# One change of three parts in a decoder step on one core: the projection's sample tile and taps, the order of the prompt attention, and the padded rows of the experts

## Time and profile before

| what | us |
|---|---|
| median of 3 runs (lowest, highest) | 1763.69 (1761.9, 1769.64) |
| the profiled execution: its own time | 1765.26 |
| the profiled execution: its span | 1763.6 |
| TensorE busy in the span | 1430.2 (81%) |
| VectorE busy | 664.6 (38%) |
| ScalarE busy | 372.2 (21%) |
| GpSimd busy | 194.4 (11%) |

### The profile page before, as it was taken

One profiled execution on the slowest core, in us unless ns is written; L12 is line 12 of the kernel. 1 busy time (PEld: TensorE's weight loads), 2 busy tenths in 40 slices (PEclk: granted clock), 3 DMA queues, 4 the chain that ended last, 5 costly groups with the idle time before them and its releaser, 6 DMA issues. The chain is left out here.

```text
span 1763.6 us, 22716 instructions
## 1 busy us (share of the span) xinstructions
PE 1430.2 (81%) x7464; PEld 835.2 (47%) x7464; DVE 664.6 (38%) x1309; ACT 372.2 (21%) x795; POOL 194.4 (11%) x348
## 2 busy tenths in 40 slices
PE   5999989558899788824499942999999999999960
PEld 4665544257755555612355521445444544454430
DVE  3597676611378566635122255000110010010007
ACT  4000111212255555520111110111111111111113
POOL 0000011253100000013000000011111111111111
PEclk9999999778679999966699975899999999999985
DMA  7500000365330000045411103999999999999927
GB/s 261 226 1 6 12 15 21 104 224 175 96 97 25 1 1 1 1 125 144 159 48 72 39 17 132 379 411 394 408 408 406 400 412 411 406 394 408 406 104 291
DMA packets 83021, 336.99 MB, mean 191 GB/s; under 512 B 9834, under 2 KB 45803, under 8 KB 64834
## 3 DMA queue, kind: packets, MB, share of 16 engines
q1 hardware_dynamic: 65130, 287.76, 42.1%
q0 software_dynamic: 15440, 47.30, 7.8%
q10 hardware_dynamic: 2384, 1.06, 0.2%
HBM read 311.20 MB, written 29.45 MB: 193 GB/s over the span
## 5 line engine op out<-in xcount | busy, mean ns | idle before, releaser
L1752 PE MATMUL ps<-arena 128*128 128x512 f32 x544 | 239.8, 597 | 0.0
L1752 PEld LDWEIGHTS ps<-arena 128*128 128x128 f32 x544 | 102.0, 190 | 136.9 <-issue 136.8
L351 PE MATMUL ps<-arena 128*128 128x512 f32 (+3 forms) x432 | 158.9, 527 | 0.0
L504 DVE SCALAR_TENSOR_TENSOR arena<-arena 128x1024 f32<-128x1024 f32 x120 | 147.7, 1283 | 1.3
L1453 PE MATMUL ps<-arena 128*128 128x512 f32 (+1 forms) x288 | 129.4, 603 | 15.8 <-DVE arena L1548 15.8
L1806 PE MATMUL ps<-arena 128*128 128x512 f32 x272 | 120.1, 593 | 7.5 <-DMA arena<-scratch_h,ints 7.5
L1760 PE MATMUL ps<-arena 128*64 128x256 f32 x1088 | 121.2, 380 | 0.0
L306 PE MATMUL ps<-arena 128*128 128x352 f32 x384 | 116.5, 464 | 4.3 <-issue 3.8
L1053 ACT ACTIVATE arena<-ps,arena 128x640 f32<-128x640 f32 (+7 forms) x128 | 90.0, 703 | 119.8 <-DVE arena L1132 103.3
L351 PEld LDWEIGHTS ps<-arena 128*128 128x128 f32 (+1 forms) x432 | 77.2, 180 | 79.4 <-issue 72.0
L964 PE MATMUL ps<-arena 128*128 128x128 f32 x528 | 82.8, 287 | 35.7 <-ACT arena L1063 32.1
(11 more groups left out here) (357 smaller groups left out, 1543.7 us busy)
## 6 DMA issues: line engine op xcount, KB each, us to landing
arena<-in_w_gate SPq DMA_DIRECT2D x34, 2048.0 KB, 11.6
arena<-in_w_up SPq DMA_DIRECT2D x34, 2048.0 KB, 16.4
arena<-in_w_down SPq DMA_DIRECT2D x34, 2048.0 KB, 16.6
arena<-in_x_prompt SPq DMA_DIRECT2D x16, 512.0 KB, 6.5
arena<-in_cache_cmp SPq DMA_DIRECT2D x64, 128.0 KB, 2.7
arena<-in_cache_cmp POOLq DMA_DIRECT2D x64, 128.0 KB, 3.2
arena<-in_cache_sel SPq DMA_DIRECT2D x64, 128.0 KB, 2.1
arena<-scratch_y SPq DMA_DIRECT2D x16, 512.0 KB, 5.5
```

What stands on the lines that cost most here:

```text
L351: mm = pe.matmul(ps[:n, b + o // 512, 0:w], xT[:, k, t * P:t * P + n], w_tm[:, k, o:o + w], start=(k == 0), stop=(k == KT_ - 1))
L504: ins = dve.scalar_tensor_tensor(o, i, dw[:, c, j:j + 1], o, ALU.mult, ALU.add)
L1752: mm = pe.matmul(ps[:, bank, :], xgT_l[:, k, :], w[LARGE][:, k, :], start=(k == 0), stop=(k == KT_ - 1))
```

## The change

Projection: the sample tile's columns are cut into four quarters of 326, each made in its own 32-column tile of TensorE, all in one bank; ScalarE copies four pieces. The 62 late taps go behind seven tiles, nine each. The state rows are copied to a place of their own after all taps, and GpSimd stores them in the compression block between its page loads of quarter 1 and the additions. Attention: chunks and the transposes back share banks 4, 5 and 7 in turn, sums use bank 6 alone; the copier of a chunk is chosen so that each half has one large copy on one engine; ScalarE does both exps before `take(2p+1)`; VectorE masks and reduces one half, then the other. Experts: empty slots get an index past the bounds (8 x 1056), and the indirect DMAs leave such rows out; the token rows' places are set to zero once; TensorE raises the first semaphores at the start of the block.

```diff
+        QTR = COLS_TM // 4
...
+                    else:
                         for k in range(KT_):
-                            mm = pe.matmul(ps[:n, b + o // 512, 0:w], xT[:, k, t * P:t * P + n],
-                                           w_tm[:, k, o:o + w], start=(k == 0), stop=(k == KT_ - 1))
+                            for q in range(4):
+                                mm = pe.matmul(ps[n * q:n * q + n, b, 0:QTR], xT[:, k, t * P:t * P + n],
+                                               w_tm[:, k, QTR * q:QTR * q + QTR], start=(k == 0),
+                                               stop=(k == KT_ - 1), tile_position=(0, n * q))
...
+                        for q in range(4):
+                            m = min(QTR, 1280 - QTR * q)
+                            act.activation(p_sb[:n, t % 2, QTR * q:QTR * q + m], ps[n * q:n * q + n, b, 0:m], ACT.Copy)
+                        logit = ps[3 * n:4 * n, b, QTR - 24:QTR]
+                    act.activation(gates[:n, t, :], logit, ACT.Sigmoid).then_inc(sem("tm_copied"), 1)
...
-                act.wait_ge(sem("qk_turned"), TILES)
-                act.activation(xin[:TAPS - 1, 0, 0:512], ps[:TAPS - 1, 0, :], ACT.Copy)
-                act.activation(xin[:NB * NS, 1, 0:512], ps[:NB * NS, 1, :], ACT.Copy)\
+                act.wait_ge(sem("tapped"), 4 * TAPS)
+                act.wait_ge(sem("sample_tapped"), 4)
+                act.activation(state_p[:TAPS - 1], ps[:TAPS - 1, 0, :], ACT.Copy)
+                act.activation(state_s[:NB * NS], ps[:NB * NS, 1, :], ACT.Copy)\
                    .then_inc(sem("state_ready"), 1)
+                act.wait_ge(sem("state_ready"), 1)
...
-                share = -(-len(late_taps) // TILES)
+                share = -(-len(late_taps) // (NQ - 1))
...
                 cmp_pages(pool, 1, 1)
+                pool.dma_start(out["out8"], state_p[:TAPS - 1]).then_inc(sem("conv_out"), 16)
+                for s in range(NS):
+                    pool.dma_start(out["out9"][:, TAPS - 1 - NS + s, :], state_s[NB * s:NB * (s + 1)])\
+                        .then_inc(sem("conv_out"), 16)
                 pool.wait_ge(sem("conv_gain_in"), 48)
...
+        def turn_bank(kind, n):
+
+            return (4, 5, 7)[turn_place[kind, n] % 3]
...
-            if keys(h // 2) > 4:
-                return "dve" if o else "act"
-            return "act" if h % 2 else "dve"
+            return "dve" if (h % 2 == 0) == (o > 0) else "act"
...
-                        if c >= 2:
-                            pe.wait_ge(sem(f"pT_{copier(c - 2)}"), copied_by(copier(c - 2), c - 2))
+                        bank_free("chunk", c)
...
-                    if r == 0 and i > 0:
-                        pe.wait_ge(sem("combined"), 2 * (i - 1) + w + 1)
+                    if r == 0 and p > 0:
+                        pe.wait_ge(sem("out_copied"), p // R)
...
                     for q in scored_at(p):
                         exp(2 * q)
+                        exp(2 * q + 1)
                     take(2 * p + 1)
-                    for q in scored_at(p):
-                        exp(2 * q + 1)
...
                     for g in range(KV):
+                        h = 2 * p + g
...
-                        ins = dve.tensor_tensor(s[:, (m - 1) * P:m * P], s[:, (m - 1) * P:m * P], con("causal"), ALU.add)
-                    chain(ins)
-                    for g in range(KV):
-                        h = 2 * p + g
-                        dve.tensor_reduce(neg_max[:, h % 4:h % 4 + 1], scores(p, g), AX.X, ALU.max, negate=True)\
+                        chain(dve.tensor_tensor(s[:, (m - 1) * P:m * P], s[:, (m - 1) * P:m * P], con("causal"),
+                                                ALU.add))
+                        dve.tensor_reduce(neg_max[:, h % 4:h % 4 + 1], s, AX.X, ALU.max, negate=True)\
                            .then_inc(sem("max_ready"), 1)
...
                 pool.indirect_dma_start(into, None, scratch_h,
-                                        bass.IndirectOffsetOnAxis(ap=ids.bitcast(U32), axis=0))\
+                                        bass.IndirectOffsetOnAxis(ap=ids.bitcast(U32), axis=0),
+                                        bounds_check=TOKENS - 1, oob_is_err=False)\
...
-            for name in ("upped0", "upped1", "downed0", "downed1", "xg_turned0", "xg_turned1"):
-                pe.sem_inc(sem(name), 1)
...
             @block.tensor
             def _(pe):
+                for name in ("upped0", "upped1", "downed0", "downed1", "xg_turned0", "xg_turned1"):
+                    pe.sem_inc(sem(name), 1)
                 pe.wait_ge(sem("counted"), 1)
...
+                dve.memset(xg_l, 0.0)
+                chain(dve.memset(xg_s, 0.0))
                 dve.wait_ge(sem("table_made"), 1)
...
+                chain(dve.tensor_scalar(empty, ps[:, 2, COLS:2 * COLS], 0.0, 8.0 * TOKENS, ALU.is_equal, ALU.mult))
+                chain(dve.memset(empty[0:1, :], 0.0))
+                dve.tensor_tensor(ints[:, 0:2 * ROUNDS], empty, ps[:, 2, 0:COLS], ALU.add).then_inc(sem("table_ready"), 1)
```

More of the change, by code:

```diff
@@ L954, in score, with bank_free @@
                     mm.then_inc(sem("scored"), 1)
+                def bank_free(kind, n):
+                    place = turn_place[kind, n]
+                    if place >= 3:
+                        before, c = turn_order[place - 3]
+                        if before == "back":
+                            pe.wait_ge(sem("combined"), c + 1)
+                        else:
+                            pe.wait_ge(sem(f"pT_{copier(c)}"), copied_by(copier(c), c))
                 def turn(h):
```

69 lines of the change are left out of this document (43 added, 26 removed).

## The result

The changed kernel takes 1723.37 us (median of 4 runs, 1722.36 to 1727.85) against 1762.80 us (4 runs on the same chip, 1756.57 to 1769.64): a ratio of 0.9772, with a 95% interval of 0.9752 to 0.9791. Its profiled execution took 1724.38 us by its own time, with a span of 1722.5 (before: 1765.26 and 1763.6). The forecast was 1723 in a range of 1706 to 1744; the time fits, but in each of its three parts a step behind the number was wrong, in the attention most of all.

What follows compares the result with a forecast made beforehand. No single bound: TensorE in projection and experts, page loads in compression, a three-engine chain in wide attention. Gains 16.2 + 10.5 + 14.5 = 41.2 off 1765.3 give 1724.1; the runs' median stands 1.6 lower: 1723, range 1706 to 1744.

Steps and rivals of the forecast that it cites:

- Sample tile: Projection's end: four column tiles run side by side, products 4.6 us instead of 17.69, bounds 4.4 and 8.1; gain 13.1.
- Stores moved: Compression block: stores in GpSimd's queue delay later page loads and TensorE's waiting product; cost 2.9 us, bounds 0 and 3.5.
- net 16.2: Projection and what follows: next block 19.1 us earlier, less 2.9 for the moved stores.
- Attention: Whole attention block: 10.5 us gained, 8.5 in the wide and 2 in the narrow part.
- Wide attention: 32 wide pairs: shorter chain gains 10.9 us, VectorE late behind copies and combines takes 2.4 back; net 8.5.
- Narrow attention: Narrow pairs: a third bank takes only the few waits for a copy; gain 2 us, bounds -2 and 5.
- Experts, start: Start of experts: weights asked for near 1066, gathers landed near 1100; products 8 us sooner, bounds 3 and 12.
- Experts, padding: Expert rounds: a third fewer rows shorten transfers some 3 us; 6.5 of 7.5 us of waits go, bounds 0 and 7.5.
- Attention nothing: Rival, attention: VectorE's extra copy and the combine eat the 0.34 us per pair; 1733 us, chance 0.13.
- Experts keep their waits: Rival, expert rounds: fixed transfer time keeps the 6.5 us of waits, 8 gained instead of 14.5; 1730 us, chance 0.11.
- no side by side: Rival, sample tile: quarters run in turn and the tile stays at 17.7 us; 1736 us, chance 0.03.
- slower by the bounds check: Rival, expert rounds: index checks lengthen GpSimd's indirect DMAs; 1.2 us more each gives 1790; chance 0.05, like waits included.

Runs made afterwards that it cites:

- stores last: Changed kernel with state-row stores behind GpSimd's last page loads and the first w_down loads held until the round's gathers: 1722.31 us, ratio 0.9762 to the kernel before.

## Why the prediction was right, and where it was not

**Sample tile: right.** 4.59 us, forecast 4.6: four column tiles run side by side, at full clock. From the products' start to the next block 19.46 us less, forecast 19.1. The nine taps a tile cost nothing: VectorE still waits 42.4 us in nine tiles for ScalarE's copies (62.5 in the earlier trace rows), and the time to the sample tile is the same within 1.1 us.

**Stores moved: forecast +2.9, no cost to be seen.** The first half of the step was right: everything behind the stores in GpSimd's queue comes 2.7 us later. The second half, "TensorE's product at 411.64 waited 6.25 us for a page, so it moves too", failed: that product starts 71.9 us into the block instead of 72.0, and the block is as long with the stores as without (means 113.8 and 113.7 us). Loads that were issued later landed no later. The net 16.2 should have been some 19.

**Attention: the size nearly, the mechanism only by half.** The distance of an ordinary pair was right: 4.99 forecast 5.03, and 0.31 less with eight tiles, forecast 0.3; the second maximum is last, right before the second exp. Wide attention 6.86 less, forecast 8.5. What failed there is the step that a combine makes VectorE 0.5 us late in five of eight cases, -2.4: no wide pair is late by it. Every fourth pair is longer than its neighbours by 0.43 (five tiles) to 1.07 (eight), some 4.8 us in eight pairs, because the transpose back takes one of three banks and the last transposes then hang on an older copy: VectorE's behind its second maximum, and with more than five tiles also ScalarE's behind both exps. I gave the shared rotation of banks no term at all, looked only at the bank of the sums ("costs nothing: the copy out ends before the next group's first product"), and missed that one more user makes every later transpose wait for an older copy. Also wrong: that the new order of masks carries the gain. It costs 3.4 us in the wide pairs, since half 0 was never last. What is left to carry it is the rule of who copies, with the third bank. Narrow attention: forecast 2 shorter, measured 1.8 longer at the same clock; the addition on VectorE costs more than that there, since 3.9 us came back without it. Attention on the whole: forecast 10.5, alone 5.1, and 5.0 against the kernel with the projection's part alone; the 7.6 between the two profiled executions is this and the clock.

**Experts, start: forecast 8, measured 6.8, for partly other reasons.** 2.7 of it is the table products, 6.27 us in place of 8.93, at a granted clock of 0.76 where it was 0.50; in the kernel with the attention's part alone, whose experts are the old ones, they took 6.20 too, so that it is not this edit's. Only 3.8 is from the early weights; about 1 goes with the left-out rows, since with all rows kept the stretch from the list to the first product is 39.2 us in place of 38.2. Two terms were missed: the weights start 2.6 us behind the list (forecast 1.5), and the step "Gathers at 1093 and 1095, landed near 1100": the first gather took 9.3 us, not 7, beside the weights, and 4.6 with nothing beside it. Holding the last two loads back gave these 4.7 us.

**Experts, padding: forecast 6.5, measured 8.8.** The waits went to zero, as said. All 8.8 us lie in the five rounds that had a wait: a round without one takes 34.30 us before and after, and those five took 35.93 to 36.19, each longer by its wait and 0.27 more, at full clock. This I had not counted. The gathers became 4 us shorter, forecast 3. The Trainium skill (DMA: Bandwidth & Descriptors, Anatomy of one DMA) would have taken some 0.4 us off a transfer, an estimate from its fixed time and its bytes at full rate. The stores agree with it (0.3 to 0.5), the gathers don't (4.0 in the median, and the fastest went from 6.5 to 2.3), and it is the gathers that TensorE waits for. Why the two differ was not tried.

**Rivals.** "Attention nothing" (1733) and the forecast are about equally far from the truth in the attention: 5 of 10.5 us came. "Experts keep their waits" fell with the zero of line 1844, "no side by side" with the 4.59 us, and "slower by the bounds check" with 0.01 to 0.06 us an issue.

By blocks the terms are 16.2, 10.5 and 14.5, sum 41.2, and measured 16.6, 7.6 (of which some 2.5 is the clock at the start) and 15.6 (2.7 the clock over the table products), with 1.2 more from blocks that no edit touches. An attention twice too high, a cost of the stores that isn't there and a clock that happened to stand higher made the sum right to half a microsecond; that closeness is luck.

## What to carry to other kernels

When a buffer is added to a rotation and a second kind of work is let into it, follow the rotation through the rarest case (here every fourth pair): each place waits for the copy three places back, on whichever engine makes it and behind whatever stands in that engine's order. Of two symmetric halves only the later one sets the pace, so an order that favours the first is worth nothing. And a short transfer that is issued beside a long stream can take twice its time or more (4.6 us alone, 9.3 to 11.3 beside the weights here): hold back the part of the stream that is not needed yet.

## What the hardware showed that I had not expected

- A wait can cost more than its length, and need not. Behind a wait of 2.30 us in the midst of full work, the next sixteen products took 8.57 us in place of 7.03, at a granted clock of 0.84 over 11 us, and behind one of 1.99 us 8.83. Waits of 2.04 and 2.12 us in another kernel, and all shorter ones, were followed by 7.13 to 7.14 us at full clock. What decides is not shown.
- The 36 table products, behind 33 us of idle time in all kernels, took 8.9 us in three (before, projection alone, stores last) and 6.2 to 6.3 in the others: 421 ns each in the median at a granted clock of 0.50, 275 ns at 0.76. The start of the attention block moves by 1.4 us in the same way. Neither goes with an edit, so that two profiled executions can differ by some 4 us with no cause in the code.
- Gathers and stores of the same rows react differently to a third fewer of them: some 4 us and 0.5 us.
- Page loads that GpSimd issued 2.7 us later landed no later: the product that waits for them starts 71.9 us into the block, 72.0 before.
